# Decays read back from DRAM as rows, and state space outputs made with channels on partitions

## What is computed

```python
gc = jnp.cumsum(g, axis=-1)
decay = jnp.exp(jnp.where(causal, gc[..., :, None] - gc[..., None, :], -jnp.inf))
...
acs = jnp.cumsum(jnp.moveaxis(adt_i, 1, -1), axis=-1)
lmat = jnp.exp(jnp.where(causal, acs[..., :, None] - acs[..., None, :], -jnp.inf))
cb = jnp.einsum("blgn,bsgn->bgls", c_i, b_i)
y_diag = jnp.einsum("bgls,bghls,bsghp->blghp", cb, lmat, xdt_i)
y_off = jnp.einsum("blgn,bghpn,bghl->blghp", c_i, state, jnp.exp(acs))
...
y = y + ssd_d.astype(f32).reshape(SSD_GROUPS, SSD_HPG)[..., None] * xs_
```

## Time and profile before

| | us |
|---|---|
| median of 3 runs | 1726.6 |
| range of the runs | 1726.42 to 1728.67 |
| the profiled execution, its own time | 1728.28 |
| its span in the trace | 1726.5 |
| PE busy | 1652.1 (96%) |
| DVE busy | 908.8 (53%) |
| ACT busy | 663.3 (38%) |
| POOL busy | 177.3 (10%) |

### The profile page before, as it was taken

One profiled execution on the slowest core, in us unless ns is written; L12 is line 12 of the kernel. 1 busy time (PEld: TensorE's weight loads), 2 busy tenths in 40 slices (PEclk: granted clock), 3 DMA queues, 4 the chain that ended last, 5 costly groups with the idle time before them and its releaser, 6 DMA issues.

```text
span 1726.5 us, 21880 instructions
## 1 busy us (share of the span) xinstructions
PE 1652.1 (96%) x8503; PEld 1342.3 (78%) x8503; DVE 908.8 (53%) x1319; ACT 663.3 (38%) x1009; POOL 177.3 (10%) x182
## 2 busy tenths in 40 slices
PE   7999999899989899999999999999999799999998
PEld 5788868778868677777788778877777688888886
DVE  5656645684644544545534647865546533333334
ACT  5444465653323433333332532444444322232221
POOL 2032203520000100000000112251000000000000
PEclk9999999999999999999999999999999899999999
DMA  7222222121125367464352322222223133332222
GB/s 198 74 66 59 65 57 61 50 75 37 38 81 193 112 204 220 153 219 159 135 166 97 98 79 62 80 65 65 64 71 123 50 97 97 96 98 98 97 97 73
DMA packets 183172, 173.82 MB, mean 101 GB/s; under 512 B 5810, under 2 KB 162561, under 8 KB 180016
## 3 DMA queue, kind: packets, MB, share of 16 engines
q1 hardware_dynamic: 179408, 163.26, 30.3%
q10 hardware_dynamic: 2528, 7.95, 1.3%
q0 software_dynamic: 1152, 1.44, 0.5%
HBM read 168.34 MB, written 4.53 MB: 100 GB/s over the span
## 4 chain that ended last, share of the span: by engine, by line
PE 66%; DVE 4%; ACT 2%; issue 1%; POOL 0%; POOLq 0%; DVEq 0%; ACTq 0%
PE acc L586 11%; PE acc L588 10%; PE acc L587 10%; PE acc L617 6%; PE acc L618 6%; PE acc L619 6%; PE acc L1115 2%; PE acc L1116 2%; PE acc L1117 2%; PE acc L631 1%; PE acc L630 1%; PE acc L629 1%; PE acc L1062 1%; PE acc L1255 1%; PE acc L1239 1%
## 5 line engine op out<-in xcount | busy, mean ns | idle before, releaser
L1943 DVE TENSOR_TENSOR w_low<-w_raw,w_high 128x1024 fp32r<-128x1024 f32 x230 | 286.9, 1248 | 618.8 <-ACT w_high L1315 618.2
L586 PE MATMUL acc<-h_high,w_high 128*128 128x512 f32 x1216 | 488.2, 401 | 11.1 <-DVE h_low L1997 3.9
L1315 ACT ACTIVATE w_high<-w_raw 128x1024 fp32r<-128x1024 f32 x224 | 237.1, 1058 | 635.7 <-PE acc L588 361.7
L588 PE MATMUL acc<-h_high,w_low 128*128 128x512 f32 x1216 | 476.5, 392 | 0.0
L587 PE MATMUL acc<-h_low,w_high 128*128 128x512 f32 x1216 | 476.2, 392 | 0.0
L586 PEld LDWEIGHTS acc<-h_high,w_high 128*128 128x128 f32 x1216 | 230.6, 190 | 86.2 <-issue 27.7
L588 PEld LDWEIGHTS acc<-h_high,w_low 128*128 128x128 f32 x1216 | 229.8, 189 | 49.4
L587 PEld LDWEIGHTS acc<-h_low,w_high 128*128 128x128 f32 x1216 | 230.8, 190 | 47.7 <-issue 1.9
L617 PE MATMUL acc<-w_high,act_high 128*128 128x512 f32 x496 | 194.2, 391 | 4.2 <-DVE arena L2621 1.5
L618 PE MATMUL acc<-w_low,act_high 128*128 128x512 f32 x496 | 193.5, 390 | 0.0
L619 PE MATMUL acc<-w_high,act_low 128*128 128x512 f32 x496 | 193.5, 390 | 0.0
(11 more groups left out here) (373 smaller groups left out, 1967.7 us busy)
## 6 DMA issues: line engine op xcount, KB each, us to landing
w_raw<-w_in SPq DMA_DIRECT2D x68, 512.0 KB, 3.7
w_raw<-w_mlp SPq DMA_DIRECT2D x64, 512.0 KB, 4.0
w_raw<-w_up SPq DMA_DIRECT2D x44, 512.0 KB, 3.9
early<-w_ada SPq DMA_DIRECT2D x22, 1024.0 KB, 6.0
w_raw<-w_out SPq DMA_DIRECT2D x24, 512.0 KB, 3.3
w_raw<-w_down SPq DMA_DIRECT2D x22, 512.0 KB, 3.3
w_raw<-w_branch_gate SPq DMA_DIRECT2D x16, 512.0 KB, 4.0
arena<-x SPq DMA_DIRECT2D x4, 512.0 KB, 5.3
```

The source lines that it names most:

```text
L586: pe.matmul(out_, wh, xh, start=start, stop=False)
L588: return pe.matmul(out_, wl, xh, start=False, stop=stop)
L1315: f(WH[:, off % 2, :], RAW[:, off % 4, :], ACT.Copy).then_inc(sem("w_high"), 1)
L1943: tt(WL[:, off % 2, :], RAW[:, off % 4, :], WH[:, off % 2, :].bitcast(F32), ALU.subtract).then_inc(sem("w_low"), 1)
```

## The change

**Spans.** After the running sums are known, PE makes them once more as rows (24 heads x 512 tokens, four matmuls), ACT copies these out of PSUM and stores them in DRAM (`gcum`), and SP reads them back, spread over all partitions: for each chunk 16 heads x 128 tokens (`state_rows`, 1 MB), for each chunk but the first eight pairs of heads with one head on either half of the partitions (`faded_rows`, two transfers of 256 KB), and for the delta rule eight times 4 heads (`delta_rows`, 256 KB each). DVE subtracts the column's running sum and clips at zero (16 `tensor_scalar` of 128 x 128 a chunk); ACT exponentiates in SBUF. For the delta rule POOL subtracts and adds -1e30 outside the causal part before the exponential. PE's span matmuls, POOL's `steps` and the mask multiplications after the exponential are gone.

**Outputs.** In `state_out` x is the stationary operand, 64 columns a head, and two heads write the two halves of the partitions. The outputs arrive with channels on partitions, `y_turn` and `y_out` are gone, the skip weight is applied in `y_sum` to the convolved x, and the outputs from the state are multiplied by the exponential of the running sums, spread by `faded_rows`.

**Order.** The delta rule's units go by twos behind blocks 32 to 35 over three pairs of PSUM banks, with four decay buffers, and none is left behind `gated(0)`.

```diff
+            def state_rows(c):
+                if c:
+                    sp.wait_ge(sem("s_diff"), 2 * c)
+                else:
+                    sp.wait_ge(sem("cum_stored"), 16)
+                sp.dma_start(E[:, 2048:4096].rearrange("p (h t) -> p h t", t=P), decay_rows(8, 16, c))\
+                    .then_inc(sem("s_rows"), 16)
...
+            def faded_rows(c):
+                if c > 1:
+                    sp.wait_ge(sem("s_y"), 2 * c)
+                for half_ in range(2):
+                    src = bass.AP(gcum.tensor, (8 + half_) * T + c * P, [[0, PD], [2 * T, 8], [1, P]])
+                    sp.dma_start(faded[PD * half_:PD * half_ + PD], src).then_inc(sem("s_faded_rows"), 16)
...
             pe.wait_ge(sem("logdec_ready"), 1)
+            for c in range(NT):
+                pe.matmul(PS[0:24, 6, c * P:(c + 1) * P], logdec[:, c, :], UPR, start=True, stop=True)
...
                 for g in range(2):
                     for h in range(8):
-                        m = pe.matmul(PS[:, 3 + 2 * g, h * PD:(h + 1) * PD], arena([QE_, R_][g] + h * P, P),
-                                      arena(TT_ + (8 * g + h) * PD, PD), start=True, stop=True)
-                    if c:
-                        m = pe.matmul(PS[:, 6 + g, :], FT[:, C0 + g, tc], arena(SS_ + g * 512, 512),
+                        at = PD * (h % 2)
+                        m = pe.matmul(PS[at:at + PD, 3 + 2 * g, h // 2 * P:(h // 2 + 1) * P],
+                                      arena(TT_ + (8 * g + h) * PD, PD), arena([QE_, R_][g] + h * P, P),
                                       start=True, stop=True)
+                    for i in range(4 if c else 0):
+                        m = pe.matmul(PS[:, 6 + g, i * P:(i + 1) * P], arena(SS_ + g * 512 + i * P, P),
+                                      FT[:, C0 + g, tc], start=True, stop=True)
...
+            act.wait_ge(sem("cum_done"), 1)
+            f(cum_rows, PS[0:24, 6, :], ACT.Copy).then_inc(sem("cum_out"), 1)
...
+            act.wait_ge(sem("cum_out"), 2)
+            act.dma_start(gcum, cum_rows).then_inc(sem("cum_stored"), 16)
...
+                if c:
+                    act.wait_ge(sem("s_faded_rows"), 32 * c)
+                    f(faded, faded, ACT.Exp).then_inc(sem("s_faded_out"), 1)
                 for g in range(2):
-                    act.wait_ge(sem("s_spans"), 2 * c + g + 1)
-                    for r in range(2):
-                        m = f(arena([QE_, R_][g] + r * 512, 512), PS[:, [5, 6, 7, 2][2 * g + r], :], ACT.Exp)
-                    m.then_inc(sem("s_exp"), 1)
+                    act.wait_ge(sem("s_diff"), 2 * c + g + 1)
+                    f(arena([QE_, R_][g], 1024), arena([QE_, R_][g], 1024), ACT.Exp).then_inc(sem("s_exp"), 1)
...
             def y_sum(c, g):
-                y, xd = arena(VN_ + g * 512, 8, PD), arena(PP_ + g * 512, 8, PD)
+                four_ = FT[:, X0 + 4 * g:X0 + 4 * g + 4, c * P:(c + 1) * P]
+                skip, old = arena(PP_ + g * 512, 4, P), arena(VN_ + g * 512, 4, P)
+                step(tt(skip, four_, up_to(skip_d[:, 4 * g:4 * g + 4], 4), ALU.mult))
...
+                dve.wait_ge(sem("s_faded_out"), c)
+                step(tt(skip, skip, by_block(3 + 2 * g), ALU.add))
+                step(tt(old, by_block(6 + g), faded[:, 4 * g:4 * g + 4, :], ALU.mult))
+                tt(four_, skip, old, ALU.add).then_inc(sem("s_y"), 1)
...
+                dve.wait_ge(sem("s_rows"), 16 * (c + 1))
+                for g in range(2):
+                    to = arena([QE_, R_][g], 8, P)
+                    for h in range(8):
+                        m = ts(to[:, h, :], rows_at(g)[:, h, :], ncum[:, c, 8 + 8 * g + h:9 + 8 * g + h], 0.0,
+                               ALU.add, ALU.min)
+                    m.then_inc(sem("s_diff"), 1)
```

More of the change, by code:

```diff
@@ L254, in arena @@
             return v
-        IDN, UPR, ONE, LOW = (C1[:, k * P:(k + 1) * P] for k in range(4))
+        IDN, UPR, ONE, NOT = (C1[:, k * P:(k + 1) * P] for k in range(4))
         FT = arena(FT_, CH, T)
@@ L279, in program @@
         head_log = small(24)
-        skip_d = small(HS)
+        skip_d = small(8)
         modT = small(NADA, 2)
@@ new lines, in _ @@
+            for i in range(8):
+                columns(CONV_N + QK_N, 1024, w_in_v)(i // 4, i % 4)
+                if i == 5:
+                    state_rows(0)
+                    faded_rows(1)
+                if i == 7:
+                    state_rows(1)
+            for i in range(8):
+                columns(CONV_N + QK_N + 8, 0, w_in_v)(i // 4, i % 4)
+                if i == 3:
+                    state_rows(2)
+                if i == 7:
+                    state_rows(3)
+                    faded_rows(2)
@@ L520, in _ @@
+            for i in range(8):
+                columns(CONV_N + V_N, 2048, w_in_v)(i // 4, i % 4)
+                if i == 3:
+                    faded_rows(3)
+            for i in range(8):
+                columns(Z_N, 4112, w_in_v)(i // 4, i % 4)
+                if i < 4:
+                    delta_rows(2 * i)
+                    delta_rows(2 * i + 1)
             blocks(sp, 8, columns(Z_N + 8, 3072, w_in_v))
@@ L727, in state_turn @@
                 m.then_inc(sem("s_turned"), 1)
-            def spans(c):
-                if c:
-                    pe.wait_ge(sem("y_turned_out"), 2 * c)
-                for g in range(2):
-                    pe.wait_ge(sem("s_steps"), 2 * c + g + 1)
-                    if g:
-                        pe.wait_ge(sem("s_x_out"), c + 1)
-                    for h in range(8):
-                        m = pe.matmul(PS[:, [5, 6, 7, 2][2 * g + h // 4], (h % 4) * P:(h % 4 + 1) * P],
-                                      steps_of(g)[:, h, :], UPR, start=True, stop=True)
-                    m.then_inc(sem("s_spans"), 1)
             def state_out(c):
                 tc = slice(c * P, (c + 1) * P)
+                if c:
+                    pe.wait_ge(sem("s_y"), 2 * c)
+                pe.wait_ge(sem("s_x"), c + 1)
                 pe.wait_ge(sem("s_m_even"), c + 1)
@@ L759, in state_out @@
                 m.then_inc(sem("s_sum"), 1)
-            def y_turn(c):
-                for g in range(2):
-                    pe.wait_ge(sem("s_y"), 2 * c + 2)
-                    for i in range(4):
-                        m = pe.transpose(PS[:, 5 + g, i * P:(i + 1) * P],
-                                         arena(VN_ + g * 512 + i * P, P), IDN)
-                    m.then_inc(sem("y_turned"), 1)
             for c in range(NT):
@@ L772, in _ @@
                 conv(n)
-                if c:
-                    y_turn(c - 1)
                 state_turn(c)
                 conv(n + 1)
-                spans(c)
                 conv(n + 2)
@@ L956, in _ @@
             conv(28)
-            y_turn(NT - 1)
             conv(29)
+            pe.wait_ge(sem("s_y"), 2 * NT)
             sums(0)
@@ L1545, in _ @@
             gated(0)
-            exps(7)
-            for u in range(3, 8):
+            for u in range(4, 8):
                 diagonal(u)
@@ L2228, in _ @@
             gated(0)
-            gram_out(7)
             dve.wait_ge(sem("d_diagonal"), 8)
```

159 lines of the change are left out of this document (63 added, 96 removed).

## The result

The changed kernel takes 1741.49 us (median of 4 runs, 1739.44 to 1745.13), the kernel before 1727.28 in the same comparison: a ratio of 1.0089, with a 95% interval of 1.0076 to 1.0103. That is 14.2 us slower, where 6 were forecast. The profiled execution took 1745.13 us, its span is 1743.3; before, the span was 1726.5, so the traces differ by 16.8. The profiled execution is the slowest of the four, so the traces differ by more than the medians. First the page of the changed kernel: its engines, and two of its transfers (KB each, us from issue to landing).

A forecast was written before the change was run, and what follows sets the result against it. PE bounds the kernel (1652.1 of 1726.5 us busy), but the DVE-ACT ring and late transfers take over: +1.1 us at full clock, 5.2 from clock drops, so +6, median 1732 us; range 1718 to 1744, likeliest 1728 to 1738.

The forecast's parts named there:

- The likeliest range: Whole kernel: ring and late transfers with most clock losses give 1728 to 1738 us, at 1732; chance 0.45.
- the fourth rival: Slow spreading: 128 partitions reading the same 8 KB take 5 us a MB, whole kernel 1737 to 1746; chance 0.18.
- Up to chunk 1: Before `state_turn(0)` +1.9 us, chunk 0 +0.7 (late rows against spans gone), chunk 1 -0.1.
- `faded_rows` 4.5 late: Chunk 2: rows land 8.8 us after issue, ACT wants them 4.3 after and stands 4.5; +4.5 us.
- rows of 512 bytes are what the weight loads move too, so I take 3.4 us a MB plus 2.1: Transfers of the rows: same rate as weight loads, so 5.5 us for 1 MB.
- 2.5 late: Chunk 2's transfer by the Trainium skill's rule, 2.0 us plus bytes at 436 GB/s: 2.5 us late, not 4.5.
- Chunk 3: Up to block 28, PE no longer waits for the state: -2.4 us, with rows 1.2 us late.
- Blocks 28 to 31 and the elimination: Blocks 28 to 31 +2.1 us, PE waiting about 5 at `sums(0)`; blocks 32 to 35 -4.3; to the merge -1.3.
- The ring: Serial hand-overs between DVE and ACT from one state update to the next: 34.8 us a chunk, against 30.6 before.
- a wait for ACT's split behind PE's block n + 1, 0.8: Item of the chunk's ring: DVE waits 0.8 us for ACT's split after the 16 differences.
- PE still sets the pace: Rival for the chunks: ring under 32 us, chunks 1 and 2 end 3 us earlier each, 1714 to 1722; chance 0.15.
- The clock: Waits of 2 us or more rise from three to nine; drops of PE's clock at 3.5 us each add 5.2 us.

The follow-up runs named there:

- early rows: Changed kernel with only SP's issue of the `faded_rows` transfers of chunks 2 and 3 moved earlier: 1729.81 us, ratio 1.0024 to the kernel before.
- kernel A: Changed kernel with `faded_rows` issued earlier and DVE's state update put between the halves of `y_sum`: 1724.48 us, ratio 0.9993 to the kernel before.
- F: kernel A plus rows by chunk, squares moved, block 28's taps and store moved, outputs begun before GpSimd's factors, GpSimd's fade after weight split: 1718.53 us, 0.9964.

## Why the prediction was right, and where not

Direction and range were right, the size was not: +14.2 us against +6. The likeliest range, 1728 to 1738, was missed. The wide one held 1741.5 only because the fourth rival stood in it, and the cause which that gave was wrong, so this part is luck. Step by step, from the rows above, in the profiled execution.

**Up to chunk 1: right.** The first turn came 1.5 us later (1.9 forecast), chunk 0 has 0.75 more (0.7), chunk 1 0.04 less (0.1 less).

**Chunk 2: the mechanism right, the term mis-sized.** The step read "`faded_rows` 4.5 late", +4.5 us. ACT waited 8.97 us and the chunk grew by 11.9. The rows were there about 12.1 us after their issue (8.8 forecast), and ACT wanted them 3.2 after it, not 4.3. Two more parts aren't in this term: DVE waited 1.79 us for the split behind the turn, at the slow clock, where it is 0.39 at full clock, 1.4 more; and 1.4 were lost where `y_sum` ran into GpSimd's fade, which the prediction doesn't have at all. The step that failed is "rows of 512 bytes are what the weight loads move too, so I take 3.4 us a MB plus 2.1": 1 MB took 10.3 us, not 5.5. The fourth rival had the sign and, with 1737 to 1746, the size, and its mark ("transfers of 1 MB over 7 us") came true. But the cause that it gave, the same 8 KB read by all partitions, fell: stored in one piece, the same reading took 6.3. With the pieces 4480 bytes apart it took 7.2, and 10.3 with 2048. The Trainium skill (DMA: Bandwidth & Descriptors, Latency and other measured facts) tells of slower copies in HBM between rows at large power-of-two distances, from 512 KiB up, and that a padding of 4 KiB brings the rate back; the runs here show slower reads at a distance of 2048 bytes than at 4480, which the page doesn't cover, and not that the power of two is the reason. The rule for one transfer in its section Anatomy of one DMA, which I had weighed (2.5 late), is fitted to transfers that GpSimd issues, and these are SyncE's; by it the miss would have been larger.

**Chunk 3: wrong sign.** Forecast -2.4 with `faded_rows` 1.2 late; measured +3.6, with 3.1 late. With timely rows the chunk has 26.32 us, 0.1 less than before. Besides ACT's wait the clock lies in it: DVE waited 2.00 us for the split behind the turn instead of 0.39, and from the start of the outputs, at the slow clock, to block 28 it is 5.61 us instead of 4.05. Without these 3.2 us and ACT's 3.10 the chunk has 23.7; the forecast, 24.0, had 1.2 of late rows in it.

**Blocks 28 to 31 and the elimination: near.** Blocks 28 to 31 took 35.0 us, 0.25 less than before, where 2.1 more were forecast; the wait at `sums(0)` was 3.5 us, not 5. The elimination starts 58.6 us after block 32 (341.55 less 282.93), 56.9 forecast. From block 32 to the merge it is 6.1 us less, against 5.6.

**The ring: right at full clock.** Chunk 1 has the 34.8 us that were summed up. The differences are 0.20 to 0.23 us apart (16 in 3.23 and 3.76) against 0.19 taken. Behind a slow turn the item "a wait for ACT's split behind PE's block n + 1, 0.8" measured 1.79 and 2.00, and 2.68 with early rows. PE waited 3.65 and 3.27 us for `s_state`, as forecast, and kernel A showed that this wait is on the path: a shorter list of DVE ahead of it gave 5.3 us. "PE still sets the pace" fell with it.

**The clock: about the right size in the changed stages, and nothing foreseen behind them.** Chunk 2 ran at 0.86 and chunk 3 at 0.89. At the turns of chunks 2 and 3, where the block behind is on the path, it cost 1.4 and 1.6 us, at chunk 3's outputs 1.6, and behind chunk 2's outputs 1.4, there only because it pushed GpSimd's fade into `y_sum`. That is 6.0 against 5.2 forecast. Behind the merge's start, where no instruction is changed, the profiled execution lost 5.5 us more (16.8 in all, 11.3 up to there). The granted clock accounts for most of it: 62.88 us of busy PE at 0.90 lose 6.3 us, 63.67 at 0.98 lose 1.3 (an estimate from the windows). In the trace of the kernel with early rows that part of the program lost 2.1 us, in that of F 0.6, so it isn't a fixed price of the change. The prediction had put every drop at a wait of the changed stages. Why the clock fell at 399 us, with PE busy from there on without a break, is open.

**Why it is slower.** The change takes 15.0 us of work from PE, which no longer sets the pace in the chunks. What does is first the rows, 11.2 us with their wait (early rows), then the list on DVE between outputs and turn (5.3), then what is left of late rows (3.3). Each of the three, measured on top of the one before, includes the clock that came back with it. With these undone the change is 0.26% faster than before, and 0.36% in F, a step that lies inside the intervals.

## What to carry to other kernels

Work that moves from TensorE to a row read back from memory has a landing time as its price: work out for each such row how long before its use it can be issued, and lay the rows so that one reader's pieces lie together; if they can't, try another distance between them. When TensorE stops being the bound, reorder the list of the engine that takes over: the result that another engine waits for goes ahead of the one that nobody waits for. After each such edit look again at which operations of VectorE and GpSimd on SBUF start together.

## What the runs showed of the hardware

- **The distance of pieces.** 1 MB in pieces of 512 bytes, read by all 128 partitions: 10.3 us with 2048 bytes from one piece to the next (9.6 to 10.3 by kernel), 7.2 with 4480, 6.3 as pieces of 8 KB. Pieces of 512 bytes each read once: 6.3 to 6.9. The two issues of chunk 2's faded rows, behind 1 MB of rows, took 5.30, 3.83 and 1.50 us in these three layouts.
- **VectorE beside GpSimd.** An operation on two SBUF tensors that began 0.08 us after GpSimd's took 2.91 instead of 1.23 us. The changed kernel has it too: `y_sum`'s first product took 2.08 us instead of 0.68, from 209.69 on, since GpSimd's fade ran from 209.32 to 211.23. The Trainium skill (SBUF — State Buffer, SBUF: two separate sides) has the rule, an exclusive lock for the whole instruction on a pair of ports, also against VectorE's operations with two SBUF inputs; the traces agree.

```profile
209.32 1.91 POOL L2761 TENSOR_TENSOR arena<-arena,small 128x1024 f32<-128x1024 f32 x1 [5.19 <-PE acc L804]
...
209.69 2.08 DVE L2122 TENSOR_TENSOR arena<-arena,small 128x512 f32<-128x512 f32 x1
```

- **The granted clock.** In the changed kernel it was 0.62 from 399 to 408 us with PE busy for all 9 us. With a wait of 10 us filled by products up to its last 3.02 us it stayed at 0.97 there, and fell during the outputs behind it. Behind the same wait of TensorE, of 3.65 and 3.67 us, it was 0.76 over the next block in the kernel with early rows, with VectorE waiting 2.68 us for the split behind it, and 1.00 in the kernel with rows 4480 bytes apart, with a wait of 0.39.
